# Exponential ahead of the copies, and one instruction for a tap's two groups: the attention stage of an encoder layer on one core

## What is computed

```python
h = rms_norm(x, attn_norm_g)
q, k, v, cv, cg = split(h @ w_in)                 # 8 query heads, 2 key/value heads of 64, 512 conv channels
q, k = rope(rms_norm(q)), rope(rms_norm(k))
attn = softmax(q @ k.T / 8) @ v                   # prompt and sample apart
u = cv * sigmoid(cg)
u = depthwise_conv(u, width 31, padding 15 | 15) + dw_b     # per channel, along the tokens
conv = silu(layer_norm(u))
x = x + concat(rms_norm(attn), rms_norm(conv)) @ w_out
x = x + expert_choice_moe(rms_norm(x))            # 16 experts, each takes its top tokens
```

## Time and profile before

| | us |
|---|---|
| median of three runs | 2613.13 |
| the profiled execution | 2615.15 |
| its span in the trace | 2613.0 |
| PE busy | 2528.8 (97%) |
| VectorE busy | 1822.8 (70%) |
| ACT busy | 1396.1 (53%) |
| GpSimd busy | 275.5 (11%) |
| mean granted TensorE clock | 0.986 of full |

### The profile page before, as it was taken

The page is one execution under the profiler, slowest core; times in us unless marked ns, Lnnn a source line. Parts: engine busy times, 40 slices in busy tenths (PEclk is TensorE's granted clock), DMA queues, the critical chain, the costliest instruction groups (busy, mean ns, idle before and its releaser), DMA issues.

```text
span 2613.0 us, 39837 instructions
## 1 busy us (share of the span) xinstructions
PE 2528.8 (97%) x15910; PEld 2337.0 (89%) x15910; DVE 1822.8 (70%) x2092; ACT 1396.1 (53%) x1762; POOL 275.5 (11%) x269
## 2 busy tenths in 40 slices
PE   8999999997995999999999999999999999999998
PEld 7889889976885999989999898998989999899997
DVE  6878899975367766667666676666767667676664
ACT  4232667677223555656556565555655556565563
POOL 3735100000000000101011010110101001010000
PEclk9999999998996999999999999999999999999999
DMA  7244000012235777878678687777868778677773
GB/s 247 99 174 164 9 1 1 1 57 90 101 110 185 234 234 238 255 231 255 224 256 247 226 260 228 251 240 240 252 223 265 236 236 255 227 257 226 247 239 124
DMA packets 339357, 499.38 MB, mean 191 GB/s; under 512 B 10225, under 2 KB 287089, under 8 KB 337265
## 3 DMA queue, kind: packets, MB, share of 16 engines
q1 hardware_dynamic: 332144, 471.76, 54.8%
q0 software_dynamic: 7040, 25.17, 3.9%
HBM read 457.05 MB, written 39.85 MB: 190 GB/s over the span
## 4 chain that ended last, share of the span: by engine, by line
PE 88%; DVE 7%; ACT 2%; POOL 1%; issue 1%; DMA 1%; SPq 0%; POOLq 0%; ACTq 0%; DVEq 0%
PE psum L1703 31%; PE psum L1705 14%; PE psum L1409 8%; PE psum L1411 8%; PE psum L1410 8%; PE psum L1726 4%; PE psum L1725 4%; PE psum L1563 4%; PE psum L1539 2%; PE psum L1550 2%; DVE conv L972 2%; DVE smx L1078 1%; DVE q_st L1067 1%; DVE top L1217 1%; DVE aff L1220 1%
## 5 line engine op out<-in xcount | busy, mean ns | idle before, releaser
L1308 DVE TENSOR_TENSOR w_lo<-raw,w_hi 128x2048 fp32r<-128x2048 f32 x384 | 880.0, 2292 | 482.9 <-ACT w_hi L858 480.4
L1703 PE MATMUL psum<-xgT,w_hi 128*128 128x384 f32 x4096 | 1168.0, 359 | 2.4 <-issue 2.4
L1705 PE MATMUL psum<-xgT,w_lo 128*128 128x192 f32 x4096 | 1026.3, 251 | 0.0
L858 ACT CAST w_hi<-raw 128x2048 fp32r<-128x2048 f32 x384 | 734.1, 1912 | 320.6 <-PE psum L1726 319.6
L1705 PEld LDWEIGHTS psum<-xgT,w_lo 128*128 128x128 f32 x4096 | 783.4, 191 | 0.6
L1703 PEld LDWEIGHTS psum<-xgT,w_hi 128*128 128x128 f32 x4096 | 769.7, 188 | 3.4 <-issue 2.8
L972 DVE SCALAR_TENSOR_TENSOR conv<-conv,colp 128x1024 f32<-128x1024 f32 (+1 forms) x240 | 252.7, 1053 | 4.8
L1409 PE MATMUL psum<-w_hi,hid_st 128*128 128x512 f32 x512 | 210.2, 411 | 0.0
L1411 PE MATMUL psum<-w_hi,hid_st 128*128 128x512 f32 x512 | 200.1, 391 | 0.0
L1410 PE MATMUL psum<-w_lo,hid_st 128*128 128x512 f32 x512 | 199.9, 390 | 0.0
L1726 PE MATMUL psum<-w_lo,hid_st 128*128 128x512 f32 x508 | 198.1, 390 | 0.0
(11 more groups left out here) (212 smaller groups left out, 3341.1 us busy)
## 6 DMA issues: line engine op xcount, KB each, us to landing
raw<-in_w_gate_dram SPq DMA_DIRECT2D x128, 1024.0 KB, 5.3
raw<-in_w_up_dram SPq DMA_DIRECT2D x128, 1024.0 KB, 5.3
raw<-in_w_down_dram SPq DMA_DIRECT2D x128, 1024.0 KB, 4.9
wi_raw<-in_w_in_dram SPq DMA_DIRECT2D x28, 256.0 KB, 5.0
wi_kept<-wi_hi SPq DMA_DIRECT2D x14, 512.0 KB, 6.3
wi_kept<-wi_lo SPq DMA_DIRECT2D x14, 512.0 KB, 6.3
wi_hi<-wi_kept SPq DMA_DIRECT2D x7, 1024.0 KB, 4.7
wi_lo<-wi_kept SPq DMA_DIRECT2D x7, 1024.0 KB, 6.9
```

Of the source, the lines that this page charges most:

```text
L858: act.copy(w_hi[:, j % SPLIT_SLOTS, :], raw[:, j % RAW_SLOTS, :]).then_inc(e_hi, 1)
L1308: dve.tensor_tensor(w_lo[:, j % SPLIT_SLOTS, :], raw[:, j % RAW_SLOTS, :], w_hi[:, j % SPLIT_SLOTS, :].bitcast(F32), ALU.subtract).then_in ...
L1703: pe.matmul(bank[:, 0:2 * CAP], w_hi[:, slot, w0:w0 + P], xgT[:, half, k, :], start=(k == 0), stop=False, skip_group_check=True)
L1705: last = pe.matmul(bank[:, 0:CAP], w_lo[:, slot, w0:w0 + P], xgT[:, half, k, 0:CAP], start=False, stop=(k == KD - 1), skip_group_check=True)
```

## The change

Three edits.

1. ACT issues `exp_unit(u + 1)` straight after `rows_unit(u - 2)`, ahead of the copies of unit u. `query_high` and `key_high` stay behind the copies.
2. The tap list is cut at `ALONE = 82`: 82 prompt taps alone, then 82 sample taps alone, then 42 taps over 1566 columns that cover prompt, gap and sample in one instruction (the gap's columns receive values that nothing reads). 42 instructions of 1024 columns and 42 of 512 become 42 of 1566. In the prompt units three sample taps run (two in a turn unit), then one wide tap, with a second one where u is a multiple of five and no turn unit. From unit 64 on what is left runs at once.
3. The conv tiles begin at unit 66, two units later, and all wait for the whole tap list.

```diff
+ALONE = 82
...
-        TAPS = [(0, c, k) for c in range(NC_CONV) for k in range(CONV_K)] + [(1, c, k) for c in range(NC_CONV) for k in range(CONV_K)]
-
-        PROMPT_TAPS = NC_CONV * CONV_K
+        PROMPT, SAMPLE, BOTH = 0, 1, 2
+        all_taps = [(c, k) for c in range(NC_CONV) for k in range(CONV_K)]
+        TAPS = ([(PROMPT, c, k) for c, k in all_taps[:ALONE]] + [(SAMPLE, c, k) for c, k in all_taps[:ALONE]] +
+                [(BOTH, c, k) for c, k in all_taps[ALONE:]])
...
-            T, base = GROUPS[g][2], GROUPS[g][3]
+            T, base = (SLOT - 2 * PAD, 0) if g == BOTH else GROUPS[g][2:4]
...
-            i = u - PROMPT_UNITS
+            i = u - PROMPT_UNITS - 2
             return i // 2 if i >= 0 and i % 2 == 0 and i // 2 < TILES else None
...
                 if u >= 2:
                     rows_unit(u - 2)
+                if u + 1 < NU:
+                    exp_unit(u + 1)
                 for hf in range(HALVES[u]):
                     m = half_no[u] + hf
                     act.wait_ge(pT, m + 1)
                     act.copy(probs_T[:, u % 2, hf * 512:(hf + 1) * 512], psum[:, ring_bank("p", m), :]).then_inc(pT_ok, 1)
-                if u + 1 < NU:
-                    exp_unit(u + 1)
                 if query_tile_at(u) is not None:
...
-                        dve.wait_ge(glu_u, glu_no[g, c, GROUPS[g][2] // 512 - 1] + 1)
+                        own = SAMPLE if g == BOTH else g
+                        dve.wait_ge(glu_u, glu_no[own, c, GROUPS[own][2] // 512 - 1] + 1)
...
-                sample_next = TAPS[min(conv_done[0], len(TAPS) - 1)][0] == 1
+                next_of = TAPS[min(conv_done[0], len(TAPS) - 1)][0]
                 if u < PROMPT_UNITS:
-                    conv_run(3 - turns if sample_next else 2 - (turns or u % 4 == 0))
-                elif u < PROMPT_UNITS + 2 * ROT_TILES - 2:
-                    conv_run(1)
+                    conv_run(3 - turns if next_of == SAMPLE else 1 + (not turns and u % 5 == 0))
                 else:
                     conv_run(len(TAPS))
...
-                pe.wait_ge(conv_tap, PROMPT_TAPS if g == 0 else len(TAPS))
+                pe.wait_ge(conv_tap, len(TAPS))
```

## The result

The changed kernel takes 2625.12 us (median of five runs, 2623.35 to 2625.46) against 2613.13 before (2611.45 to 2614.36): a ratio of 1.0043, 95% interval 1.0032 to 1.0054. It is 12.0 us slower by the medians. The profiled execution took 2625.19, with a span of 2623.1, 10.1 above the span before.

A forecast was written before the change was run, and what follows sets the result against it. PE was taken as full in plain prompt units, with 0.24 us slack on the reciprocal's chain. Prompt with opening +14.6 and sample -4.1 gave +10.5 on 2615.15, 2625.7; for the median 2623.6, range 2615 to 2630.

The forecast's parts named there:

- PE is full and the chain through the reciprocal decides: Prompt's plain units: PE 100% busy at 3.59 us; a reciprocal over 0.24 us late loses PE time for good.
- The wide tap, 1.80: VectorE: a 1566-column tap takes 1.80 us, bounds 1.255 and 2.00; one in a unit is hidden.
- Two wide taps together, 1.21 each and 1.95 for unit 30: Units 35, 40, 45, 50, 55, 60 lose 1.21 us each, unit 30 with a sample tap 1.95; sum +9.2.
- The exponential ahead of the copies in plain units, nothing: ACT in plain units: copies end at 4.55, ahead of the reciprocal at 4.59; worth nothing, costs nothing.
- The same in turn units, +3.8, +1.1 and +3.1: Copies join the turn units' chain: four isolated query turns +3.8 us, two key turns +1.1, the opening +3.1.
- Prompt taps gone, -2.2: Early prompt units: eighteen units no longer lose 0.12 us each to two 1024-column taps, -2.2.
- The sample, -4.1: Seven of twelve unit pairs lose their taps, 5.21 to 4.55 us, -4.6; two units without a tile +0.5.
- The conv tiles' loads, nothing: w_out's loads end two units later, some 4 us off a lead of 29; counted as nothing.
- the first: Attention stage: late reciprocals up to 2 us still leave PE fed, so it is faster, 2602.8 us; chance 6%.
- The second: Only the turns cost: wide tap near 1.255 us gives 2616.0, pairs wholly absorbed 2614.4; chance 12%.
- The third: Opening's turns 1 to 4: PE's clock stays at half speed, 2.5 us more four times, 2634; chance 7%.
- The fourth: Taps don't fuse as meant, or the sample gains nothing because ACT's order is on its chain; 2628, chance 5%.

The follow-up runs named there:

- e2: The changed kernel with never two wide taps in one unit, the last 8 wide taps left out of the computation; 2614.54 us, ratio 1.0003 to the kernel before.
- e1: The changed kernel with ACT's old order put back (exponential of unit u + 1 behind the copies of unit u), wide taps kept; 2617.22 us.
- e5: The changed kernel with the turned tile's casts between the exponential and the copies, the exponential still first; 2615.20 us.
- e3: The changed kernel with ACT's old order and never two wide taps in a unit, the last 8 left out; 2607.99 us.
- e7: The kernel before with the 14 taps of units 64 to 77 put two by two in the odd units, without a conv tile; 2610.57 us.
- e8: The kernel before with casts ahead of the exponential in turn units and the sample's taps two by two in odd units, nothing left out; 2605.14 us.
- e9: e8 with the exponential ahead of the copies in the sample's units (64 to 95) alone; 2606.49 us, ratio 0.9970 to the kernel before.

## Why the prediction was right

It forecast 2623.6 for the median, and 2625.1 was measured; 10.5 us of loss, and 12.0 by the medians, 10.1 by the spans. The total and the mechanism hold; some of its terms were off and cancelled. Point by point:

- **PE is full and the chain through the reciprocal decides.** Right. Its slack of 0.24 us is 0.08 too large, 0.16 by its own sum (see e2). The costs were taken from the sum and not from the slack, and e2's unit 30 (0.17 by the sum, 0.15 lost) meets it. The weighted product starts 0.65 behind a late reciprocal in the changed kernel as it did in the earlier trace rows.
- **The wide tap, 1.80.** It starts every 1.82 (two in 3.64). The line through two rows held; its bounds, 1.255 and 2.00, weren't needed. The formula set beside it from the Trainium skill ("VectorE: DVE Perf Modes", the section on the TRN2 errata) is given there for an fp32 add of two tensors. For this operation it is close at the wide end only: 0.743 at 512 columns, 1.255 at 1024 and 1.82 at 1566, against 0.69, 1.22 and 1.79 as estimates by the formula. The half throughput that the prediction takes from the Trainium skill ("Vector Engine (DVE) Microarchitecture Reference", Points that are easy to get wrong), an estimate of 3.4, is refuted by the 1.82; by the prediction's sum such a tap alone would have lost 1.0, not 1.1.
- **Two wide taps together, 1.21 each and 1.95 for unit 30.** 1.24 and 2.03; e2 took all seven away and the rest fell by 9.3, where the sum had 9.2.
- **The exponential ahead of the copies in plain units, nothing.** Right: plain units keep 3.59, also with one wide tap.
- **The same in turn units, +3.8, +1.1 and +3.1.** The isolated query turns lost 1.83 over plain units (1.85 foretold), the opening 3.1 at equal clock. But before the change a query turn had lost 1.02 and not the 0.89 of the sum, so in the changed kernel the four cost 0.8 more each and not 0.96. The key turn behind a pair of wide taps (u = 36) compounds with it, 2.26 for the two units, and 1.21 + 1.01 had been added up. e1 and e5 show that it is the order, and e5 that it is the copies' place in it.
- **Prompt taps gone, -2.2.** 2.3 in e3, but 18 units at 0.12 is not how it comes about. Sixteen units held two prompt taps. Nine of them lost 0.12 (3.71 in place of 3.59), the four directly behind a turn 0.25 (3.84 and 3.85), and the three ahead of a turn nothing. The count and the size were both off and cancelled. Units 8 to 15 take 3.59 in the changed kernel, and the whole of this stretch came out at 223.4 for 223.2.
- **The sample, -4.1.** It is -4.2, but in part by luck. The twelve pairs of units with a conv tile take 3.65 less (57.95 before, from unit 66 to 90; 54.30 after, from unit 68 to 92) where 4.6 was foretold: only six of the seven pairs with taps had cost 5.21, the first 4.33. The units without a tile were to take 0.5 more and take 0.6 less (23.72 before, 23.13 after). Why they do is not shown. A smaller error lies in the order. I said that ACT's order wasn't on the sample's chain. In the units with a squares instruction it is, by 0.13 a pair on average: with the old order those pairs take 4.73 (e7), with the new one 4.61 on average in the changed kernel (18.42 for four, unit 70 to 78). My flat 4.55 for all pairs is nearer to the new order; for e7, which has the old one, it was 0.7 us too good over the four.
- **The conv tiles' loads, nothing.** The loads are issued 25.2 us ahead of their first read (590.71 to 615.87), 29.3 before; no wait for them appeared.

```profile
590.71 3.37 SPq L476 DMA_DIRECT2D wo_raw<-in_w_out_dram  x7
```

```profile
615.87 1.03 ACT L785 CAST wo_hi<-wo_raw 128x1024 fp32r<-128x1024 f32 x1
```

Of the rivals, the first (losses absorbed, VectorE's sum of work decides) is refuted: the sum fell and the time rose, and e2 regained 9.3 for 14.6 of work removed. The second (a wide tap near 1.255) is refuted by its 1.82. The third (PE's clock stays at half speed through turns 1 to 4) didn't occur: from 286 us on the clock is full, and the opening was longer by the 3.1 that the chain gives. The fourth (the sample gains nothing) neither; that ACT's order lies on its chain is true, but it shortens the sample.

The medians moved by 1.5 us more than foretold. The profiled executions moved by 10.0, as the chain has it. Executions of one and the same kernel spread over 5 us here (2611.35 to 2616.39 for the kernel before in 31 runs), so I take nothing from that difference. That the profiled pair agrees so well is helped by both having been granted the same clock in the opening; at full clock the opening is 0.8 to 0.9 shorter.

## What to carry to other kernels

Where one engine is full and the others feed it, put a number on the slack of each feeding chain, and place side work so that no unit goes over it: the same taps cost nothing in one unit and their excess, to the tenth of a microsecond, in another, and fusing them into fewer and longer instructions removes work but makes them harder to place. Before moving an instruction ahead on an in-order engine, list what stands behind the place it jumps over; here the gain was for the exponential, which nobody waited for, and the cost fell on the casts, which somebody did. Side work goes where the engine already waits for the full one: for the taps of the sample that was the unit without a conv tile.

## What the runs showed of the hardware that I had not expected

**The clock that PE is granted in the opening differs between executions of the same code.** e8 and e9 have the same instructions up to the end of the prompt's turns, and their opening took 30.47 and 28.64 us. Busy time by engine (columns as in rows 1), e8:

```profile
276.00:280.00 4.00, 2.35 (x14) 2.25 (x15) 2.77 (x3) 2.75 (x5) 0.00 (x0) 0.84 0.00 0
280.00:284.00 4.00, 3.20 (x13) 2.38 (x13) 3.76 (x4) 2.48 (x5) 0.00 (x0) 0.50 0.00 0
284.00:288.00 4.00, 4.00 (x27) 3.78 (x25) 1.69 (x5) 3.16 (x6) 0.00 (x0) 0.81 0.00 0
```

and e9:

```profile
276.00:280.00 4.00, 2.14 (x15) 1.55 (x14) 3.58 (x3) 2.06 (x4) 0.00 (x0) 0.89 0.00 0
280.00:284.00 4.00, 2.33 (x17) 1.81 (x17) 3.18 (x4) 3.20 (x7) 0.00 (x0) 1.00 0.00 0
```

In e8 the clock had risen (0.84 on the mean from 276 to 280 us), fell back to half (1.2 of 2.4 GHz) from 280 to 284 us, and rose again; in e9 it stayed at full clock. The time from unit 2's scores to unit 3's, which lies there, is 7.63 in e8 (279.14 to 286.77) and 5.91 in e9 (279.74 to 285.65), nearly all of the 1.8 us by which the openings differ. That is a third of what a measurement of this kernel can tell from no change, and it is why effects of 1 us had to be read from stretches of the trace that lie behind the opening.
